# Three transformer blocks on one core: where the modulation columns are made, and how the first projections and tokens are loaded

## The reference, cut to what matters

```
def hybrid_layer(x, w_in, ...):              # block 1, twice
    proj = jnp.einsum("bld,de->ble", x, w_in)
    q, k, v, z_attn, z_ssm, xbc, dt_raw = jnp.split(proj, IN_SPLITS, axis=-1)
    ...
    dt = jax.nn.softplus(dt_raw + dt_bias)
    out = jnp.einsum("ble,ed->bld", jnp.concatenate([attn, ssm], axis=-1), w_out)
    return layer_norm(DEEPNORM_ALPHA * x + out, ln_g, ln_b)

# block 3, what is called modulation here
    c_3 @ w_ada_3 + b_ada_3                  # 1024 -> 3072: shift, scale, gate
    un * norm_w_3 * (1 + scale) + shift      # 256 tokens, columns of 128 channels
```

## Time and profile before

| what | us |
|---|---|
| median of 3 runs | 2086.45 |
| the runs | 2087.86, 2086.45, 2079.56 |
| the profiled execution, its own time | 2075.69 |
| its span in the profile | 2074.0 |
| PE busy | 1695.1 (82%) |
| DVE busy | 563.0 (27%) |
| ACT busy | 294.3 (14%) |
| POOL busy | 11.5 (1%) |
| PE line 675 and line 686 (modulation), busy | 14.1 and 5.5 |

### The profile page before, as it was taken

One profiled execution on the slowest core, in us unless ns is written; L12 is line 12 of the kernel. 1 busy time (PEld: TensorE's weight loads), 2 busy tenths in 40 slices (PEclk: granted clock), 3 DMA queues, 4 the chain that ended last, 5 costly groups with the idle time before them and its releaser, 6 DMA issues.

```text
span 2074.0 us, 21120 instructions
## 1 busy us (share of the span) xinstructions
PE 1695.1 (82%) x9180; PEld 1031.2 (50%) x9180; DVE 563.0 (27%) x1306; ACT 294.3 (14%) x783; POOL 11.5 (1%) x35
## 2 busy tenths in 40 slices
PE   8999999999999999866566766656667575899888
PEld 6675477645488886532123323321223231468754
DVE  0473414633341412411111111111011110116552
ACT  0243303422112100100100000000000001112220
POOL 0000000000000000000000000000000000000000
PEclk9999999999999999897888878888788888999989
DMA  9442263348253374699999999999999999544100
GB/s 348 140 99 76 83 222 122 122 130 276 89 203 122 125 270 160 270 428 427 428 428 428 427 427 428 427 427 427 427 428 427 427 428 394 195 162 163 41 1 21
DMA packets 106614, 553.35 MB, mean 267 GB/s; under 512 B 7856, under 2 KB 10416, under 8 KB 82960
## 3 DMA queue, kind: packets, MB, share of 16 engines
q1 hardware_dynamic: 105664, 548.81, 66.9%
q0 software_dynamic: 848, 3.05, 0.4%
HBM read 550.79 MB, written 1.05 MB: 266 GB/s over the span
## 4 chain that ended last, share of the span: by engine, by line
PE 66%; DMA 24%; DVE 6%; ACT 3%; issue 1%; SPq 0%; DVEq 0%; ACTq 0%
PE bank L629 34%; DMA ring<-in_w 13%; DMA arena<-in_w 10%; PE bank L1084 7%; PE bank L1057 6%; PE bank L638 5%; PE bank L1105 5%; PE bank L617 2%; ACT arena L1456 1%; PE bank L846 1%; DVE arena L1951 1%; PE bank L675 1%; PE bank L780 1%; PE bank L760 0%; DMA ring<-in_w_in 0%
## 5 line engine op out<-in xcount | busy, mean ns | idle before, releaser
L629 PE MATMUL bank<-arena,ring 128*128 128x256 f32 x1856 | 413.8, 381 | 2.7 <-DVE arena L2768 2.2
L1084 PE MATMUL bank<-ring,arena 128*32 128x512 f32 x1216 | 283.5, 728 | 152.9 <-DMA ring<-in_w 98.9
L629 PE MATMUL bank<-ring,arena 128*128 128x512 f32 (+5 forms) x1000 | 381.2, 536 | 15.2 <-ACT arena L1380 3.0
L629 PEld LDWEIGHTS bank<-arena,ring 128*128 128x128 f32 x1856 | 350.8, 191 | 54.2 <-issue 7.2
L1084 PE MATMUL bank<-arena 128*32 128x512 f32 x832 | 232.9, 724 | 97.5 <-DMA ring<-in_w 51.8
L629 PEld LDWEIGHTS bank<-ring,arena 128*128 128x128 f32 x1000 | 186.9, 198 | 181.6 <-issue 150.9
L1084 PEld LDWEIGHTS bank<-ring,arena 128*32 128x32 f32 x1216 | 72.0, 131 | 283.4 <-issue 283.4
L1057 PE MATMUL bank<-arena 128*128 128x128 f32 x512 | 126.4, 421 | 29.7 <-DVE arena L2480 28.6
L1057 PEld LDWEIGHTS bank<-arena 128*128 128x128 f32 x512 | 123.4, 335 | 43.4 <-DVE arena L2480 41.3
L1084 PEld LDWEIGHTS bank<-arena 128*32 128x32 f32 x832 | 58.2, 130 | 174.0 <-issue 173.8
L1105 PE MATMUL bank<-ring,arena 128*32 128x512 f32 x608 | 109.6, 594 | 6.8 <-ACT arena L1666 6.8
(11 more groups left out here) (368 smaller groups left out, 1220.0 us busy)
## 6 DMA issues: line engine op xcount, KB each, us to landing
ring<-in_w SPq DMA_DIRECT2D x114, 2048.0 KB, 31.1
arena<-in_w SPq DMA_DIRECT2D x78, 2048.0 KB, 30.8
ring<-in_w_in SPq DMA_DIRECT2D x42, 2048.0 KB, 8.1
ring<-in_w_out SPq DMA_DIRECT2D x6, 2048.0 KB, 7.9
ring<-in_w_ada SPq DMA_DIRECT2D x6, 2048.0 KB, 8.1
ring<-in_w_out SPq DMA_DIRECT2D x16, 512.0 KB, 9.2
ring<-in_w_conv_out SPq DMA_DIRECT2D x2, 2048.0 KB, 8.5
ring<-in_w_attn_out SPq DMA_DIRECT2D x2, 2048.0 KB, 7.8
```

The costliest lines, as they stand in the source:

```text
L629: i = te.matmul(ps, lhsT, rhs, start=n0 + k == 0, stop=n0 + k == n - 1)
L1084: m = te.matmul(ps[32 * j:32 * j + 32, :], LM.xg[:, f, 128 * k + 32 * j:128 * k + 32 * j + 32], vs[j][:, 512 * (k % 2):512 * (k % 2) + 512 ...
```

## The change

1. **Modulation.** The matmuls of `prm` columns by weights are gone from PE. POOL takes each of the six weight tiles in its ring buffer (128 partitions x 8 chunks x 512 columns), multiplies it in place by the `c_3` columns, adds the eight chunks pairwise in three steps (2048, 1024, 512 elements per partition), and writes 512 sums per partition to one of two buffers `ada` (the second lies in `wr`, unused until block 2). PE then sums over partitions: four matmuls with the buffer's 128 columns as weights and one column of ones. DVE adds the bias. Three tiles are done in layer 0 and three in layer 1; PE's parts stand behind the turn of `sT` for tile 0, behind that for tile 1, and behind the turn of the next block's first tile.
2. **Loads of `w_ada_3`** are spread over both layers by the table `ADA`; POOL, not PE, marks them `used`.
3. **dt behind v.** v's 256 and dt's 16 columns lie side by side in one ring tile and are one product of 272 columns; k is a tile of its own (1 MB).
4. **Tokens in two transfers**, one a tile, and only the constants of layer 0 early (behind k); the rest go behind zs of layer 0.
5. **Seven matmuls** of the identity by itself on PE at the very start, whose result nobody reads.

```diff
-def layer_order(ly):
+def layer_order():
...
-            if att_on and na < 46 and (na < 5 or done >= 18):
+            if att_on and na < 46 and (na < 5 or done >= 16):
...
-        for _ in range(1 if done == 20 else 0 if done < 36 else 2 if ns in (8, 11, 13, 16) else 1):
+        for _ in range(1 if done == 18 else 0 if done < 34 else 2 if ns in (8, 11, 13, 16) else 1):
...
-    n_proj = 42 + (3 if ly else 0) + 8
+    n_proj = 40 + 8
...
+        ada = [ar(22336, 512), wr[:, :, :].rearrange("p a b -> p (a b)")[:, 0:512]]
+
+        ADA = {("oa", 0, 0): 0, ("oa", 0, 1): 1, ("os", 0, 0): 2, ("q", 1, 1): 3, ("za", 1, 1): 4, ("zs", 1, 1): 5}
...
-            le.dma_start(h[:, :, :], x[0].rearrange("(t p) d -> p t d", p=128)).then_inc(h_sem, 16)
...
+            for tt in range(2):
+                le.dma_start(h[:, tt, :], x[0, 128 * tt:128 * tt + 128]).then_inc(h_sem[tt], 16)
+                at.put(("h", -1, tt), h_sem[tt], 16)
+            wad = w_ada_3[0].rearrange("(c p) n -> p c n", p=128)
+
+            def layer_load(name, *srcs, **kw):
+                if name in ADA:
+                    n = ADA[name]
+                    load(("ada", n), (whole, wad[:, :, 512 * n:512 * n + 512]))
+                load(name, *srcs, **kw)
...
-                load(("dt", ly), (whole, wv[:, :, 5120:5136]), width=16)
-                load(("kv", ly), (whole, wv[:, :, 1024:1536]))
+                load(("vd", ly), (lambda v: v[:, :, 0:256], wv[:, :, 1280:1536]),
+                     (lambda v: v[:, :, 256:272], wv[:, :, 5120:5136]), width=272)
+                load(("k", ly), (whole, wv[:, :, 1024:1280]), width=256)
+                if ly == 0:
+                    le.dma_start(prm[:, PK1[0]:PK1[0] + 132], pk1[0]).then_inc(prm_sem, 16)
...
+            def modulation(n, b):
+
+                ps = fresh("mod", n, b=b)
+                t.wait_ge(*at.of("ada", n))
+                for k in range(4):
+                    i = te.matmul(ps[:, k:k + 1], ada[n % 2][:, 128 * k:128 * k + 128], ones[:, 0:1], start=True, stop=True)
+                i.then_inc(*t.done("mm", "mod", n))
...
+                if ly == 0:
+
+                    t.wait_ge(*at.of("const"))
+                    for _ in range(7):
+                        te.matmul(P[0][:, 0:128], ident[:, :], ident[:, :], start=True, stop=True)
...
-                    t.wait_ge(*at.of("w", ("dt", ly)))
+                    t.wait_ge(*at.of("w", ("vd", ly)))
                     ready(*both("hT", ly, tt))
-                    tok(("dt", ly, tt), hT, dt, tt, 16)
+                    tok(("vd", ly, tt), hT, weights(("vd", ly), 272), tt, 272)
...
-                if ly:
-                    yield from modulation()
...
                         turn_T(("sT", ly), L1.y, 0)
+                        modulation(3 * ly, None)
...
                 turn_T(("sT", ly), L1.y, 1)
+                modulation(3 * ly + 1, 0)
                 out_ssm(1)
...
+                modulation(3 * ly + 2, 2)
...
+            def modulation(n):
+                c_n, c_b, k = PK3, PK3 + 16, 4 * n
+                v.wait_ge(*at.of("mm", "mod", n))
+                v.wait_ge(*at.of("prm", 1))
+                ps = bank("mod", n)
+                if n < 4:
+                    ve.tensor_tensor(mod[:, k:k + 4], ps[:, 0:4], prm[:, c_b + k:c_b + k + 4], ALU.add
+                                     ).then_inc(*v.done("ev", "mod", n))
+                else:
+                    ve.tensor_copy(mod[:, k + 8:k + 12], ps[:, 0:4]).then_inc(*v.done("ev", "mod", n))
...
                 turned(("sT", ly), L1.ssmT, 1, scale=prm[:, C_N:C_N + 8])
+                modulation(3 * ly + 1)
                 layer_norm(ly, 0)
...
+                modulation(3 * ly + 2)
                 layer_norm(ly, 1)
...
+            def modulation(n):
+
+                to, w = ada[n % 2], weights(("ada", n))
+                ready(("w", ("ada", n)), ("prm", 1), *([("mm", "mod", n - 2)] if n > 1 else []))
+                ge.tensor_tensor(w, w, bc(col1(prm[:, PK3 + 8:PK3 + 16]), 512), ALU.mult).then_inc(*p.step())
+                for c in (4, 2):
+                    p.wait_ge(*p.last())
+                    ge.tensor_tensor(w[:, 0:c, :], w[:, 0:c, :], w[:, c:2 * c, :], ALU.add).then_inc(*p.step())
+                p.wait_ge(*p.last())
+                ge.tensor_tensor(to, w[:, 0, :], w[:, 1, :], ALU.add).then_inc(*p.done("ada", n))
+                p.also("used", ("ada", n))
```

More of the change, by code:

```diff
@@ L240, in program @@
         unit_sem = [sem(f"unit{i}_loaded") for i in range(10)]
-        h_sem, prm_sem, ln_sem, side_sem, router_sem, out_sem = (
-            sem(n) for n in ("h_loaded", "prm_loaded", "ln_loaded", "side_loaded", "router_loaded", "out_stored"))
+        h_sem = [sem(f"h{tt}_loaded") for tt in range(2)]
+        prm_sem, later_prm_sem, ln_sem, side_sem, router_sem, out_sem = (
+            sem(n) for n in ("prm_loaded", "later_prm_loaded", "ln_loaded", "side_loaded", "router_loaded", "out_stored"))
         NG, NG0 = 20, 16
@@ L477, in sync_program @@
                 for g in range(2):
-                    load(("zs", ly, g), (whole, wv[:, :, 2560 + 512 * g:3072 + 512 * g]))
-                if ly:
-                    wad = w_ada_3[0].rearrange("(c p) n -> p c n", p=128)
-                    for n in range(6):
-                        load(("ada", n), (whole, wad[:, :, 512 * n:512 * n + 512]))
+                    layer_load(("zs", ly, g), (whole, wv[:, :, 2560 + 512 * g:3072 + 512 * g]))
+                if ly == 0:
+                    le.dma_start(prm[:, PK1[1]:PK1[1] + 132], pk1[1]).then_inc(later_prm_sem, 16)
+                    le.dma_start(prm[:, PK2:PK2 + 304], pk2).then_inc(later_prm_sem, 16)
+                    le.dma_start(prm[:, PK3:PK3 + 381], pk3).then_inc(later_prm_sem, 16)
+                    le.dma_start(posi[:, :], pos3).then_inc(later_prm_sem, 16)
+                    at.put(("prm", 1), later_prm_sem, 64)
@@ L483, in sync_program @@
                 for n in range(2):
                     ns = slice(512 * n, 512 * n + 512)
-                    load(("oa", ly, n), *[(lambda v, a=a, kp=kp: v[64 * a:64 * a + 64, 4 * kp:4 * kp + 4, :],
-                                           wo[0:1024, ns].rearrange("(k a g d) n -> k a d g n", k=2, a=2, g=4)[kp, a])
-                                          for a in range(2) for kp in range(2)])
+                    layer_load(("oa", ly, n), *[(lambda v, a=a, kp=kp: v[64 * a:64 * a + 64, 4 * kp:4 * kp + 4, :],
+                                                 wo[0:1024, ns].rearrange("(k a g d) n -> k a d g n", k=2, a=2, g=4)[kp, a])
+                                                for a in range(2) for kp in range(2)])
@@ L663, in both @@
                 return [("ev", *name, j) for j in range(2)]
[L665 to L689, removed]
@@ L711, in layer_proj @@
                     if i:
[L712 removed]
+                        t.also("used", ("k", ly))
                     yield
@@ L1447, in layer_proj @@
                         yield
-                for _ in range((3 if ly else 0) + 8):
+                for _ in range(8):
                     yield
@@ L1883, in log1p_exp_neg_abs @@
                 ve.tensor_tensor(dst, dst, w1, ALU.mult).then_inc(*v.step())
[L1885 to L1907 removed]
+            def modulation(n):
[8 more added lines that the diff above has]
+                    ve.tensor_copy(mod[:, k + 8:k + 12], ps[:, 0:4]).then_inc(*v.done("ev", "mod", n))
+                if n == 5:
+                    ve.scalar_tensor_tensor(mod[:, 16:24], mod[:, 8:16], 1.0, prm[:, c_n:c_n + 8], ALU.add, ALU.mult
+                                            ).then_inc(*v.done("mod"))
             def layer_proj(ly):
@@ L2114, in layer_ssm @@
                         turned(("sT", ly), L1.ssmT, 0, scale=prm[:, C_N:C_N + 8])
+                        modulation(3 * ly)
                         yield
@@ L2883, in gpsimd_program @@
                 at.put(("ln", "loaded", ly), ln.sem, ln.n)
+                for n in range(3 * ly, 3 * ly + 3):
+                    modulation(n)
             sd = Slot(side_sem)
```

84 lines of the change are left out of this document (23 added, 61 removed).

## The result

The changed kernel takes 2098.93 us, median of 4 runs (2097.4 to 2100.59), the kernel before 2085.97 (4 runs, 2079.56 to 2087.86). The ratio is 1.0072, 95% interval 1.0051 to 1.0093: 0.7% slower, where 1.3% faster was forecast. The profiled execution took 2097.4 us (span 2095.7), 21.7 over the span of before. The profiled run of before is 10 us under its median and that of after 1.5, so the two traces are compared stretch by stretch and the medians as medians.

The account below looks back on a forecast made before the run. PE was taken to bound block 1, with the experts' DMA stream following it. Terms -22.0 - 1.1 - 5.5 + 1.0 = -27.6 us against the median 2086.45 gave 2058.9 us, 1.3% less; range 2047 to 2073.

Parts of the forecast that it names:

- The modulation off PE: Layer 1 of block 1: taking the modulation's matmuls off PE saves 22.0 us, between 19.1 and 22.9.
- The bound of four uncovered groups: Low end of the layers' saving, -19.1 us: PE's short matmul groups there cost 0.92 each, hidden by no wait.
- The start: Before layer 0's first q product: earlier weights and merged v and dt start q 5.5 us sooner, between 4.5 and 8.9.
- Rival (b): At the kernel's start, the first 272-column product runs at full speed: 2055.5 us, chance 0.12.
- The boundary: Between layers 0 and 1: PE waits for the norm but the merged product is shorter; -1.1 us, bounds -1.6 and +3.6.
- POOL's new work: Beside PE, mainly tiles 0 and 1 in layer 0: slowing DVE costs 1.0 us, between nothing and 8.7.
- Rival (a): POOL gets in DVE's way in two stretches of layer 0: upper bound 2066.6 us, chance 0.15.
- the sign that I gave: If layer 0 from q to `hT` exceeds 230 us, check DVE's line 1951, 256-element form, 0.485 us before.
- the other reading: POOL's time per weight tile at 2.0 ns an element, 15.4 us, instead of the 13.0 used.
- (c): The experts' weight stream sets the end whatever comes before: no gain, 2086 us, chance 0.05.
- (d): Saved work turns into waits, in the buffer ring and between layers, for half the gain: 2073 us, chance 0.04.
- (e): Slower: POOL's long work on tile 2 delays tile 3's load and q's second tile in SP's queue; 2100 us, chance 0.04.

Follow-up runs that it names:

- the run with the boundary filled: Changed kernel with all six POOL tiles moved to quiet places, plus 14 identity matmuls on PE while it waits for the norm between layers; 2053.64 us, ratio 0.9873.
- the run with tile 1 alone: Changed kernel with POOL's arithmetic kept only for weight tile 1, in layer 0, and the other five tiles only cleared; 2069.04 us.

## Why the prediction was wrong

**The modulation off PE, -22.0.** Right. Without POOL's arithmetic layer 1 takes 231.2 us against 252.8, so 21.6. (The bound of four uncovered groups adds up to -19.2, not -19.1; nothing hangs on it.)

**The start, -5.5.** Right in its steps: -6.0 in the trace. The weights landed at 9.3 as worked out, and the first product was slow. It took 6.65 where I had 7.1. Rival (b), full speed behind the seven matmuls, did not come; it came near (3.93) only where the wait was filled too. The trace gives the clock of this stretch in some runs only (0.54 from 9.6 to 11.5 in the run with the boundary filled, but 1.00 in the changed kernel, whose product took 6.65), so at the start the clock is inferred from the durations.

**The boundary, -1.1.** It came to +1.7. I saw that PE would wait for the norm, and put the slow clock only among the bounds (+3.6). It was the likely case: PE idled 3.4 us and then the turn and the product together took 2.9 us longer, and 2.6 to 3.1 in all seven traces whose gap is open. The runs with the gap filled take this back.

**POOL's new work, +1.0 with +8.7 as the upper bound.** This is the step that failed, by 45 us. Two parts of it were wrong. First the mechanism: for the bound I let both engines slow to half speed while they overlap, so that an 0.485 us instruction of DVE would cost 0.485 more, and I chose a value near nothing because POOL's instructions are so much longer that both "must take turns somehow rather than one stand still". In fact one stands still: DVE's instruction is held to the end of POOL's, 6.04 us for one of 0.17, some 7 for one of 0.485. The bound has to be taken from the length of POOL's instruction, not of DVE's: the whole of POOL's time in the stretch where DVE is on the chain, so 15 to 16 us a tile. For the three tiles in layer 0 alone that would have made 46. Second the reach: I counted 18 conv instructions and left out the copies and scalings of eight elements and the mask products, which are held as well; tiles 2 and 5 cost 9.7 and 8.0 in stretches for which I had asked only when POOL would be done. Rival (a) named the right engine pair and the first two stretches, but with this price, and the sign that I gave (layer 0 over 230, line 1951 of the kernel before over 0.485) pointed to the place: 0.81 on average. POOL's time, 13.0 us a tile, was 15.2 undisturbed: the additions with two full inputs take 2.2 ns an element (2048 in 4.50), where I used 1.56, the slope between two short rows. The 15.4 that I gave as the other reading was right.

The Trainium skill, GPSIMD Engine Reference, Key points, names contention with DVE instructions that have two SBUF inputs or run in a 2-port perf mode. The runs agree on the two-input forms (7.18 us for 0.49 beside a POOL product). They also show copies and scalings inside SBUF held (7.12), and whether these run in such a mode no view names. The price, half speed, was my own guess; the measured one is the rest of POOL's instruction.

**Rivals.** (c), the experts' stream setting the end, is refuted: without POOL's arithmetic block 1 ends 45.3 us earlier by the traces and the kernel 44.3, 46.5 by the medians. (d) and (e) named the ring; SP did wait once, 56.9 us, for POOL to release a buffer, and PE waited for no weights behind it. The true way to slower, to which I gave 0.04, was (a) at its right price.

## What to carry to other kernels

Before elementwise work goes to POOL, list what DVE does at the same time. Of the eight forms measured here, those with two inputs from SBUF and the copy and scaling inside SBUF wait for the POOL instruction in progress, while those that read a bank, the reduction and the reciprocal do not. Put long POOL work where DVE only empties banks, and cut it small where that can't be had: the first was worth 41 of the 46 us here, the second 25. When an idle PE has a slow product behind it, look at the granted clock; independent matmuls in the gap can be worth more than they cost (2.5 us here).

## What was not expected of the hardware

- The profile books the hold as busy time of the held instruction: DVE's mean for a 256-element `scalar_tensor_tensor` rises from 0.485 to 2.8 us beside tile 1 (three in 8.38), and no wait names POOL.
- POOL's scaling by a column (10.6 us for 4096 elements) is slower than its product with a broadcast input (7.0), and both hold DVE. Its copy takes 3.60, its clearing 3.51.
- The product behind the boundary took 5.91 us after 3.44 us of idle, and 6.72 after 2.73 with a turn that was almost at speed (1.20). The length of the gap doesn't tell the two apart: in the run with tile 1 alone the gap was 3.43, the turn took 1.09 and the product 6.85. Turn and product together took 7.6 to 8.0 us in all seven traces. Why the clock falls sooner or later stays open; that filling the gap removes both is shown.
- Seven matmuls at the very start, followed by a turn and 2.4 to 3.6 us of idle, left the first product between 5.62 and 6.75 us. With the idle filled it took 3.93.
